# A two-block transformer in one kernel: attention's turns and scores inside units, memory units split ahead of a norm, a third query unit ahead of the keys' turn

## The chip, the cores and the metric

The kernel runs on one core of one Trainium2 chip. The metric is the device time in microseconds (us) of one execution, the median of several; three executions of the kernel before gave 1648.68, 1643.34 and 1647.32 us, median 1647.32 us.

## The reference, cut to what matters

The input is 256 tokens of width 1024, all float32. Two blocks follow each other.

- The first block has two layers (here L = 0 and 1). Each has a mixer with three branches on one input projection (a long convolution by spectra, differential attention with 4 heads, pooling), an output projection, a layer norm, a mixture of experts with a gated side path, and a second layer norm.
- The second block has two layers (here 2 and 3). Layer 2 mixes by a gated MLP with a spatial product. Layer 3 is a latent attention: projected and normed queries of 512, projected and normed keys and values of 256, 8 heads of 192 (128 plain and 64 rotated), causal. Both also attend to a memory of 256 rows, whose keys and values come from one product, `rms_norm(mem) @ w_mem_kv`, taken once. Both end in an RMS norm and a mixture of experts.

```
# differential attention, layers 0 and 1
probs = softmax(q1 k1) - lam * softmax(q2 k2);  heads = probs @ v
# memory, once
mem_kv = rms_norm(mem, g) @ w_mem_kv
# latent attention, layer 3
q = rms_norm(rms_norm(h @ w_q) @ w_q_up);  kv = rms_norm(h @ w_kv) @ w_kv_up
```

## The kernel before, in words

**Units.** All weights come as units of 1 MB (less in layer 3), 128 partitions by 2048. SyncE loads them in their order of use into a ring of 4 buffers (`RAW`); the load of a unit waits until VectorE has done with the unit four ahead of it. A float32 product is made of three fp32r products, so every unit is split: ScalarE copies it to a rounded high part (`w_hi`, L1423), VectorE subtracts that from the raw values to get the low part (`w_lo`, L1980), each in two halves (`split`). The parts have 3 buffers; ScalarE's `split` waits until TensorE has used the unit three before. TensorE takes a unit in `unit_by_token` (24 matmuls of 512 columns, L633 to L635) or `unit_by_channel` (48 matmuls of 256 columns, L679 to L681 and L633 to L635); it waits for the first half ahead of chunk 0 and for the second ahead of chunk 2. A callback `mid` runs in `unit_by_token` between chunks 1 and 2.

**Order.** Nothing plans at run time. Each engine's instruction list is written out by hand in one function for that engine, and it is worked off strictly in that order, with semaphores between the engines. On TensorE the 8 PSUM banks have owners: `claim(bank)` waits for the signal of whoever reads the bank last.

**Turns.** `turn` on TensorE transposes blocks into a bank (L650); ScalarE copies it out rounded (`t_hi`, L1429), VectorE subtracts for the low part (`t_lo`, L1992).

**Attention, layers 0 and 1.** Scores come in four rounds r = 0 to 3: `scores(r)` on TensorE (L948, banks 4 and 5 for even r, 6 and 7 for odd), `negmax(r)` on VectorE (L2471, L2474), `exponential(r)` on ScalarE (L1624), `weigh(r)` on VectorE (L2482 to L2488: the two softmaxes combined), `turn_probs(r)` on TensorE (L961), `probs_t(r)` on ScalarE (L1632: copies the transposed probabilities out). `scores(2)` needs the bank that `probs_t(0)` frees, `scores(3)` the one that `probs_t(1)` frees. TensorE's order before is: scores 0 and 1; the first unit of the third convolution strip; turn 0; scores 2; the second unit of that strip; turn 1; scores 3; a unit of the values strip; turn 2; the transposes of the convolution's input (L1066); the pooling products (L1075); the second unit of the values strip; turn 3. ScalarE's `conv_b` step (L1614) waits for the end of the second unit of the third convolution strip.

**Memory units, start of layer 2.** Four units carry `w_mem_kv`. TensorE works them as two strips (`strip((4, 5), ...)`, `strip((2, 3), ...)`, L1207 and L1208), then turns the normed activations (`turn(("n1", 2), ...)`, L1209) and starts layer 2's own units. Between the splits of these units VectorE makes layer 1's last norm (`shift_and_scale`, L2072, four instructions of 1024 columns), measures the result (L2045) and makes the RMS norm `n1` (`finish_rms`, L2063). It keeps the memory keys and values at L2677 and L2684, which wait for TensorE's second and fourth unit.

**Layer 3.** `unit_kv(0)` and `unit_kv(1)` make keys and values, `unit_q(0)` to `unit_q(3)` the queries, in 384 columns each, alternating between banks 0, 1 and 2, 3. ScalarE and VectorE work each in one `query_strip(i)`: copy the bank out, square it, sum the squares. TensorE's order before is: query unit 0, memory probabilities turn 0, query unit 1, turn 1, memory values 0, `k_nope` (the keys' turn, four groups in banks 5, 7, 5, 7), memory values 1, `k_rope`, query unit 2, the memory heads' turn, the first half of the queries' turn, query unit 3, scores. VectorE's `tables()` builds the rotation tables and also turns the 64 rotated key columns (L2816 to L2819), ahead of the copy of the memory queries (`z_m`, L2838).

Of the kernel before, what the change touches and what calls it, by code (L numbers as in the profile page):

```python
# [15 lines left out]
ALU = mybir.AluOpType  # L16
# [5 lines left out]
TB = T // P  # L22
# [114 lines left out]
def program(nc, A, seen):  # L137

    ctx = ExitStack()
    with ctx:  # L140
# [482 lines left out]
        def _(pe):  # L623
# [45 lines left out]
            def unit_by_channel(cells, pool_bank, first, last):  # L669

                pe.wait_ge(split_half[0], s.count(1))
                for c in range(4):
                    if c == 2:
                        pe.wait_ge(split_half[1], s.count(1))
# [256 lines left out]
            for L in range(DEPTH):  # L931
# [120 lines left out]
                turn_probs(0)  # L1052
                scores(2)
                unit_by_channel(cells_b, 3, False, True)
                owner[2], owner[3] = dve_ready.at(("conv_b", L)), evac_a.at(("pool", L))
                turn_probs(1)
                scores(3)
                claim(0, 1)
                unit_by_token((0, 1), lambda c: c, True, False)
# [245 lines left out]
            def unit_q(i):  # L1305
                banks = (2 * (i % 2), 2 * (i % 2) + 1)
                claim(*banks)
                unit_by_token(banks, lambda c: c, True, True, 384)
                owner[banks[0]], owner[banks[1]] = evac_a.at(("q_up", i)), evac_d.at(("q_up", i))
# [5 lines left out]
            mem_values(3, 0, ATC, 4)  # L1315
            turn("k_nope", lambda h: KV[:, :, 256 * h:256 * h + P], 8, [dve_ready.at("k")], low=False, banks=(5, 7))
            mem_values(3, 1, ATC, 6)
            turn("k_rope", KRP, 4, [], low=False, banks=(5, 7))
            unit_q(2)
# [92 lines left out]
        def _(act):  # L1412
# [184 lines left out]
            for L in range(DEPTH):  # L1597
# [71 lines left out]
                exponential(2)  # L1669
# [7 lines left out]
                split()  # L1677
                exponential(3)
# [81 lines left out]
            split()  # L1760
            root(("n1", 2), 2)
            split()
# [118 lines left out]
            split(4 * 384)  # L1881
            mem_probs_t(3, 0, ATC, (4, 5))

            def query_strip(i):
# [8 lines left out]
                act.nop().then_inc(*evac_a.tick(("q_up", i)))  # L1893
                act.wait_ge(*evac_d.at(("q_up", i)))
# [32 lines left out]
            query_strip(0)  # L1927
            mem_probs_t(3, 1, ATC, (6, 7))
            query_strip(1)
            turn("k_nope", 8, KTN, banks=(5, 7), scale=GNK[:, 2:3])  # L1930
            turn("k_rope", 4, KTR, banks=(5, 7))
            query_strip(2)
# [3 lines left out]
            query_strip(3)  # L1936
# [27 lines left out]
        def _(dve):  # L1964
# [424 lines left out]
            for L in range(DEPTH):  # L2389
# [142 lines left out]
                convolve("conv_a", range(4), lambda j: j // 2)  # L2532
                negmax(2)
                split()
# [135 lines left out]
            done("mem_root")  # L2670
            shift_and_scale(X, ("ln2", 1))
            done(("ln2", 1))
            measure(X)
            finish_rms(("n1", 2), None, GROW1, ("norm1", 2), split)
            split()
# [130 lines left out]
            def tables():  # L2806
# [6 lines left out]
                sync()  # L2813
                k1, k2 = ZB[:, :, 768:800], ZB[:, :, 800:832]
# [21 lines left out]
            done("tables")  # L2836
            used(first, 5)
            copy(ZB[:, 1, 832:1344], BK[1][:, :], "z_m")  # L2838
            turn("cq", 4, TH, TL, banks=(5, 6))
            split()  # L2840
# [14 lines left out]
            split(4 * 384)  # L2855
            mem_negmax(3, 0, (4, 5))
# [6 lines left out]
            variance("k")  # L2863
            split(4 * 384)
# [8 lines left out]

            def query_strip(i):

                used(first, 8 + i)
                b = 2 * (i % 2) + 1
                copy(QQ[:, 1, 384 * i:384 * i + 384], BK[b][:, 0:384], ("q_up", i))
                dve.wait_ge(*act_ready.at(("ssq", 4 + i)))
                go(dve.tensor_reduce(SQS[:, :].rearrange("p (b h) -> p b h", b=TB)[:, :, 2 * i:2 * i + 2],  # L2880
                                     SCR[:, :].rearrange("p (b n) -> p b n", b=TB)[:, :, 0:384]
                                     .rearrange("p b (h c) -> p b h c", c=192), X_AXIS, ALU.add))
                done(("ssq", i))
# [47 lines left out]
            query_strip(0)  # L2931
            split(4 * 384)
            mem_heads(3, 0, 4, CATM)
            query_strip(1)
            rotate(0)
            mem_heads(3, 1, 6, CATM)
            query_strip(2)
            turn(("heads_m", 3), 4, TH[:, 4:8, :], TL[:, 4:8, :], banks=(4, 6))
            split()
            query_strip(3)  # L2940
# [109 lines left out]
```

## Time and profile before

| | |
|---|---|
| median of three executions | 1647.32 us |
| the profiled execution | 1646.45 us |
| its span in the trace | 1644.4 us |
| TensorE busy | 1523.8 us (93%) |
| VectorE busy | 1316.9 us (80%) |
| ScalarE busy | 1029.5 us (63%) |
| mean granted TensorE clock | 0.973 of full |
| DMA, mean | 244 GB/s |

A row of the timeline gives the start, the duration, the engine, the line, the operation with its tiles and the number of instructions merged; in brackets stands how long the engine had been idle before it and what ended that. A busy matrix engine is not one at its peak, and the ends of its matmuls are modelled. The granted clock is 1.0 (2.4 GHz) or 0.5 (1.2 GHz); a mean between them says how much of a stretch was at either.

### The profile page before, as it was taken

The page shows a single profiled execution, that of the slowest core. Times are in us where ns is not written, and L with a number is a line of the kernel's source. Part 1 is how long each engine was busy: PE and PEld are TensorE (multiplying, and loading weights), DVE is VectorE, ACT ScalarE, POOL GpSimd, SP SyncE. Part 2 cuts the span into 40 slices and gives each one's busy share as a digit, 9 for nine tenths or more (in the row PEclk, how much of TensorE's full clock was granted, in tenths as well). Part 3 has the DMA queues.
Part 4 walks back from the last instruction along what each step waited for, and adds up shares of the span by engine and source line. Part 5 has one row for each costly group of instructions (what it writes and reads, how often), then busy time and mean ns, then how long its engine had stood idle before and what let it go on. Part 6 is the DMA issues. An engine that isn't in the chain of part 4 may idle for free.

```text
span 1644.4 us, 21331 instructions
## 1 busy us (share of the span) xinstructions
PE 1523.8 (93%) x7238; PEld 1245.9 (76%) x7238; DVE 1316.9 (80%) x1945; ACT 1029.5 (63%) x1499; POOL 94.3 (6%) x185
## 2 busy tenths in 40 slices
PE   7999999979899999989969999999789969999998
PEld 4777877858778778768858888887677758788886
DVE  5767899887678999866677999988875568899897
ACT  3544677745546777547436777776575437777775
POOL 4002000030022000000200000000000200000000
PEclk9999999989999999999979999999999979999999
DMA  8533599965437899745537999999441419999996
GB/s 280 163 109 121 183 336 348 332 213 192 138 105 225 296 340 332 263 156 166 169 104 241 360 360 360 362 321 353 153 146 60 132 52 306 350 361 359 361 333 232
DMA packets 307455, 401.79 MB, mean 244 GB/s; under 512 B 16028, under 2 KB 220540, under 8 KB 307092
## 3 DMA queue, kind: packets, MB, share of 16 engines
q1 hardware_dynamic: 298500, 382.00, 70.2%
q0 software_dynamic: 8848, 18.43, 3.9%
q8 instruction: 58, 0.95, 0.2%
q14 instruction: 49, 0.40, 0.1%
HBM read 399.33 MB, written 1.05 MB: 243 GB/s over the span
## 4 chain that ended last, share of the span: by engine, by line
PE 73%; DVE 16%; ACT 5%; DMA 4%; issue 2%; DVEq 0%; SPq 0%; ACTq 0%; POOLq 0%
PE bank L633 20%; PE bank L635 19%; PE bank L634 19%; DVE w_lo_at L1980 6%; DMA raw_at<-in_moe_w_up_dram 2%; PE bank L650 2%; ACT w_hi_at L1423 2%; PE bank L773 1%; PE bank L800 1%; PE bank L938 1%; DMA raw_at<-in_moe_w_dram 1%; DVE x_at L2355 1%; DVE t_lo_at L1992 1%; DVE x_at L2010 1%; DVE x_at L2016 1%
## 5 line engine op out<-in xcount | busy, mean ns | idle before, releaser
L1980 DVE TENSOR_TENSOR w_lo_at<-raw_at,w_hi_at 128x1024 fp32r<-128x1024 f32 (+1 forms) x730 | 853.8, 1212 | 102.5 <-ACT w_hi_at L1423 93.4
L1423 ACT ACTIVATE w_hi_at<-raw_at 128x1024 fp32r<-128x1024 f32 (+1 forms) x730 | 726.8, 1046 | 176.0 <-PE bank L635 79.2
L633 PE MATMUL bank<-w_hi_at,xs_hi_at 128*128 128x512 f32 x800 | 325.7, 407 | 15.3 <-DVE w_lo_at L1980 7.6
L635 PE MATMUL bank<-w_hi_at,xs_lo_at 128*128 128x512 f32 x800 | 316.4, 395 | 0.0
L634 PE MATMUL bank<-w_lo_at,xs_hi_at 128*128 128x512 f32 x800 | 314.1, 393 | 0.0
L633 PE MATMUL bank<-w_hi_at,t_hi_at 128*128 128x512 f32 (+3 forms) x528 | 208.2, 394 | 14.4 <-DVE t_lo_at L1992 8.5
L635 PE MATMUL bank<-w_hi_at,t_lo_at 128*128 128x512 f32 (+3 forms) x528 | 201.6, 382 | 0.0
L634 PE MATMUL bank<-w_lo_at,t_hi_at 128*128 128x512 f32 (+3 forms) x528 | 201.5, 382 | 0.0
L633 PEld LDWEIGHTS bank<-w_hi_at,xs_hi_at 128*128 128x128 f32 x800 | 151.6, 189 | 47.9 <-DVE w_lo_at L1980 9.5
L635 PEld LDWEIGHTS bank<-w_hi_at,xs_lo_at 128*128 128x128 f32 x800 | 151.5, 189 | 35.3
L634 PEld LDWEIGHTS bank<-w_lo_at,xs_hi_at 128*128 128x128 f32 x800 | 152.1, 190 | 30.7
L633 PE MATMUL bank<-w_hi_at,act_hi_at 128*128 128x512 f32 x384 | 154.2, 402 | 3.9 <-DVE act_lo_at L2244 3.9
L634 PE MATMUL bank<-w_lo_at,act_hi_at 128*128 128x512 f32 x384 | 151.6, 395 | 0.0
L635 PE MATMUL bank<-w_hi_at,act_lo_at 128*128 128x512 f32 x384 | 151.4, 394 | 0.0
L633 PEld LDWEIGHTS bank<-w_hi_at,t_hi_at 128*128 128x128 f32 x528 | 100.8, 191 | 39.3 <-issue 18.0
L635 PEld LDWEIGHTS bank<-w_hi_at,t_lo_at 128*128 128x128 f32 x528 | 100.8, 191 | 18.6
L634 PEld LDWEIGHTS bank<-w_lo_at,t_hi_at 128*128 128x128 f32 x528 | 101.0, 191 | 16.8 <-issue 0.5
L633 PEld LDWEIGHTS bank<-w_hi_at,act_hi_at 128*128 128x128 f32 x384 | 72.2, 188 | 24.6 <-issue 7.0
L635 PEld LDWEIGHTS bank<-w_hi_at,act_lo_at 128*128 128x128 f32 x384 | 72.4, 189 | 17.2
L634 PEld LDWEIGHTS bank<-w_lo_at,act_hi_at 128*128 128x128 f32 x384 | 72.5, 189 | 15.5
L1496 ACT ACTIVATE act_hi_at<-bank 128x256 fp32r<-128x256 f32 x96 | 36.6, 381 | 61.3 <-PE bank L800 60.9
L1429 ACT ACTIVATE t_hi_at<-bank 128x512 fp32r<-128x512 f32 x47 | 26.3, 596 | 61.7 <-PE bank L650 61.7
(505 smaller groups left out, 1734.7 us busy)
## 6 DMA issues: line engine op xcount, KB each, us to landing
raw_at<-in_moe_w_dram SPq DMA_DIRECT2D x192, 512.0 KB, 5.9
raw_at<-in_moe_w_gate_dram SPq DMA_DIRECT2D x128, 512.0 KB, 5.9
raw_at<-in_moe_w_up_dram SPq DMA_DIRECT2D x128, 512.0 KB, 7.6
raw_at<-in_moe_w_down_dram SPq DMA_DIRECT2D x128, 512.0 KB, 6.2
raw_at<-in_w_in_dram SPq DMA_DIRECT2D x40, 512.0 KB, 5.5
raw_at<-in_a_w_in_dram SPq DMA_DIRECT2D x20, 512.0 KB, 4.6
raw_at<-in_w_out_dram SPq DMA_DIRECT2D x16, 512.0 KB, 4.2
raw_at<-in_ple_wg_dram SPq DMA_DIRECT2D x16, 512.0 KB, 5.7
```

What stands on the lines that cost most here:

```text
L633: pe.matmul(out, ah, bh, start=start, stop=False, skip_group_check=loose)
L634: pe.matmul(out, ah, bl, start=False, stop=False, skip_group_check=loose)
L635: return pe.matmul(out, al, bh, start=False, stop=stop, skip_group_check=loose)
L650: ins = pe.transpose(BK[b][:, c * T + tb * P:c * T + tb * P + P], block_, IDENT)
L773: ins = pe.matmul(BK[2 * tb + half][:, :], ST[:, tb * P:(tb + 1) * P], y[:, half * 512:half * 512 + 512], start=first and y is YH, stop=False,
L800: ins = pe.transpose(BK[6 + e % 2][:, f * P:(f + 1) * P], GLU[:, f * P:(f + 1) * P], IDENT)
L938: ins = pe.matmul(out, mat[:, kb, cols], rhs(kb), start=kb == 0, stop=kb == 1)
L1423: act.activation(WH[:, s.part(), a], RAW[:, s.slot(), a], ACT.Copy).then_inc(hi_half[i], 1)
L1429: act.activation(dst[:, 2 * g:2 * g + 2, :], BK[banks[g % len(banks)]][:, :].rearrange("p (c t) -> p c t", c=2), ACT.Copy, scale=scale)\
L1496: act.activation(AH[e % 2][:, :, :], BK[6 + e % 2][:, 0:256].rearrange("p (c t) -> p c t", t=P), ACT.Copy).then_inc(*m.ah.tick())
L1980: dve.tensor_tensor(WL[:, s.part(), a], RAW[:, s.slot(), a], WH[:, s.part(), a].bitcast(F32), ALU.subtract).then_inc(split_half[i], 1)
L1992: dve.tensor_tensor(dl[:, 2 * g:2 * g + 2, :], BK[banks[g % len(banks)]][:, :].rearrange("p (c t) -> p c t", c=2), dh[:, 2 * g:2 * g + 2, ...
```

## The change

In the attention of layers 0 and 1, `turn_probs(0)` moves into the middle of the second convolution unit, `scores(2)` behind that unit, and `scores(3)` into the middle of the first values unit. ScalarE makes `exponential(2)` behind the next split instead of ahead of `conv_b`; VectorE makes its next split ahead of `negmax(2)`. At the start of layer 2, both split the third and the fourth memory unit earlier: VectorE one ahead of `shift_and_scale` and one ahead of `measure`, ScalarE both ahead of `root(("n1", 2), 2)`. In layer 3, `unit_q(2)` moves ahead of `k_nope`; `query_strip` is cut into `query_block` (copy out and first square) and `query_squares` (second square, sum); and the rotated keys move out of `tables()` to behind the turn of `cq`.

```diff
             def unit_by_channel(cells, pool_bank, first, last, mid=None):
...
                 for c in range(4):
+                    if c == 2 and mid is not None:
+                        mid()
...
# TensorE, layers 0 and 1
-                turn_probs(0)
+                unit_by_channel(cells_b, 3, False, True, mid=lambda: turn_probs(0))
+                owner[2], owner[3] = dve_ready.at(("conv_b", L)), evac_a.at(("pool", L))
                 scores(2)
-                unit_by_channel(cells_b, 3, False, True)
-                owner[2], owner[3] = dve_ready.at(("conv_b", L)), evac_a.at(("pool", L))
                 turn_probs(1)
-                scores(3)
                 claim(0, 1)
-                unit_by_token((0, 1), lambda c: c, True, False)
+                unit_by_token((0, 1), lambda c: c, True, False, mid=lambda: scores(3))
                 turn_probs(2)
# TensorE, layer 3
             mem_values(3, 0, ATC, 4)
+            unit_q(2)
             turn("k_nope", ...)
             mem_values(3, 1, ATC, 6)
             turn("k_rope", KRP, 4, [], low=False, banks=(5, 7))
-            unit_q(2)
# ScalarE, layers 0 and 1
                 probs_t(0)
-                exponential(2)
                 (conv_b, pool)
                 probs_t(1)
                 split()
+                exponential(2)
                 exponential(3)
# ScalarE, start of layer 2
             root(("ln2", 1), 4)
             split()
+            split()
             root(("n1", 2), 2)
-            split()
# ScalarE, layer 3
-            split(4 * 384)
-            mem_probs_t(3, 0, ATC, (4, 5))
...
+            query_block(0)
+            mem_probs_t(3, 0, ATC, (4, 5))
+            split(4 * 384)
+            query_squares(0)
             mem_probs_t(3, 1, ATC, (6, 7))
-            query_strip(1)
+            query_block(1)
+            query_squares(1)
+            query_block(2)
             turn("k_nope", 8, KTN, banks=(5, 7), scale=GNK[:, 2:3])
             turn("k_rope", 4, KTR, banks=(5, 7))
-            query_strip(2)
+            query_squares(2)
# VectorE, layers 0 and 1
+                split()
                 negmax(2)
-                split()
                 convolve("conv_b", (4, 5), lambda j: 2)
# VectorE, start of layer 2
             done("mem_root")
+            split()
             shift_and_scale(X, ("ln2", 1))
             done(("ln2", 1))
+            split()
             measure(X)
-            finish_rms(("n1", 2), None, GROW1, ("norm1", 2), split)
-            split()
+            finish_rms(("n1", 2), None, GROW1, ("norm1", 2))
# VectorE, layer 3
             tables()
-            done("tables")
             used(first, 5)
             copy(ZB[:, 1, 832:1344], BK[1][:, :], "z_m")
             turn("cq", 4, TH, TL, banks=(5, 6))
+            turned_keys()
+            done("tables")
...
             variance("k")
+            query_block(0)
             split(4 * 384)
             rooted("k", 16)
...
-            query_strip(0)
+            query_squares(0)
             split(4 * 384)
             mem_heads(3, 0, 4, CATM)
-            query_strip(1)
+            query_block(1)
+            query_squares(1)
             rotate(0)
+            query_block(2)
             mem_heads(3, 1, 6, CATM)
-            query_strip(2)
+            query_squares(2)
```

## Rows read from the trace of the kernel before

**Rows 1.** The page, the chain that ended last, by engine.
```profile
PE 73%; DVE 16%; ACT 5%; DMA 4%; issue 2%; DVEq 0%; SPq 0%; ACTq 0%; POOLq 0%
```

**Rows 2.** TensorE by stretch: length, busy (count), granted clock, DMA share, GB/s.
```profile
73.40:79.40 6.00, 6.00 (x50) 1.00 0.86 294
85.30:92.90 7.60, 7.60 (x50) 0.74 0.21 71
420.20:427.50 7.30, 7.30 (x50) 0.77 0.12 20
704.70:718.40 13.70, 13.70 (x48) 0.79 0.85 291
722.40:733.40 11.00, 10.97 (x48) 1.00 0.45 143
```

**Rows 3.** Timeline of TensorE, attention of layer 0.
```profile
80.35 0.66 PE L961 MATMUL bank<-consts_at,probs_a_at 128*128 128x128 f32 x4 [0.92 <-DVEq L2490]
83.33 2.08 PE L948 MATMUL bank<-qkt_at 64*128 64x256 f32 x8 [2.32 <-ACT at_a_at L1632]
95.17 1.13 PE L948 MATMUL bank<-qkt_at 64*128 64x256 f32 x8 [1.65 <-ACT at_a_at L1632]
96.24 0.50 PE L633 MATMUL bank<-w_hi_at,t_hi_at 128*128 128x512 f32 x1
101.82 0.60 PE L961 MATMUL bank<-consts_at,probs_a_at 128*128 128x128 f32 x4
```

**Rows 4.** Timeline of TensorE, attention of layer 1.
```profile
416.05 0.66 PE L961 MATMUL bank<-consts_at,probs_a_at 128*128 128x128 f32 x4 [0.78 <-DVEq L2490]
419.12 1.13 PE L948 MATMUL bank<-qkt_at 64*128 64x256 f32 x8 [2.41 <-ACT at_a_at L1632]
```

**Rows 5.** Timeline of ScalarE, attention of layer 0.
```profile
80.79 2.00 ACT L1423 ACTIVATE w_hi_at<-raw_at 128x1024 fp32r<-128x1024 f32 x2 [0.18 <-ACT probs_a_at L1624]
82.70 0.58 ACT L1632 ACTIVATE at_a_at<-bank 128x512 f32<-128x512 f32 x1
```

**Rows 6.** Timeline of VectorE, attention of layer 0.
```profile
82.44 3.35 DVE L2498 SCALAR_TENSOR_TENSOR uc_at<-bank,cols_at,uc_at 128x255 f32<-128x255 f32 x8
97.00 0.17 DVE L2482 RECIPROCAL r_at<-su_at 128x2 f32<-128x2 f32 x1 [0.17 <-DVE vvt_at L2536]
98.79 1.29 DVE L2471 TENSOR_REDUCE mx_at<-bank 128x2 f32<-128x512 f32 x2
```

**Rows 7.** The chain in order of time: one round of exponentials.
```profile
78.67 1.94 ACT probs_a_at L1624 x8
```

**Rows 8.** Timeline of TensorE, memory units and first unit of layer 2.
```profile
704.66 0.79 PE L633 MATMUL bank<-w_hi_at,xs_hi_at 128*128 128x512 f32 x1 [5.63 <-DVE w_lo_at L1980]
722.43 0.49 PE L633 MATMUL bank<-w_hi_at,t_hi_at 128*128 128x512 f32 x1 [2.11 <-DVE t_lo_at L1992]
```

**Rows 9.** Timeline of VectorE, start of layer 2.
```profile
694.81 2.48 DVE L2072 SCALAR_TENSOR_TENSOR x_at<-x_at,mv_at,row_at 128x1024 f32<-128x1024 f32 x2 [0.18 <-DVE rs_mem_at L2669]
703.38 2.36 DVE L1980 TENSOR_TENSOR w_lo_at<-raw_at,w_hi_at 128x1024 fp32r<-128x1024 f32 x2 [0.22 <-DVE rs_at L2039]
718.61 0.75 DVE L2684 TENSOR_SCALAR mem_v_at<-bank,rs_mem_at 128x512 f32<-128x512 f32 x1 [4.53 <-PE bank L635]
719.82 2.48 DVE L1992 TENSOR_TENSOR t_lo_at<-bank,t_hi_at 128x512 fp32r<-128x512 f32 x4 [0.46 <-ACT t_hi_at L1429]
```

**Rows 10.** Timeline of TensorE, layer 3.
```profile
1197.72 0.47 PE L633 MATMUL bank<-w_hi_at,t_hi_at 128*128 128x512 f32 x1 [1.17 <-DVE zb_at L2617]
1232.06 1.97 PE L650 MATMUL bank<-consts_at,kv_at 128*128 128x128 f32 x8 [3.82 <-ACT ktn_at L1429]
1245.47 0.63 PE L650 MATMUL bank<-consts_at,qrp_at 128*128 128x128 f32 x4 [1.78 <-DVE t_lo_at L1992]
```

**Rows 11.** Timeline of ScalarE, the keys' turn of layer 3.
```profile
1231.34 1.25 ACT L1429 ACTIVATE ktn_at<-bank,gnk_at 128x512 f32<-128x512 f32 x2
```

**Rows 12.** Who waited for whom: us in total, times, longest.
```profile
ACT w_hi_at L1423 <- DMA raw_at<-in_moe_w_up_dram: 38.2, 63, 2.3
```

More of the change, by code:

```diff
@@ L667, in unit_by_token, with unit_by_channel @@
                 s.unit += 1
-            def unit_by_channel(cells, pool_bank, first, last):
+            def unit_by_channel(cells, pool_bank, first, last, mid=None):
                 pe.wait_ge(split_half[0], s.count(1))
                 for c in range(4):
+                    if c == 2 and mid is not None:
+                        mid()
                     if c == 2:
@@ L1880, in _, with query_block @@
             root("k", 16)
-            split(4 * 384)
-            mem_probs_t(3, 0, ATC, (4, 5))
-            def query_strip(i):
+            def query_block(i):
                 used(first, 8 + i)
@@ L1893, in query_strip, with query_squares @@
                 act.nop().then_inc(*evac_a.tick(("q_up", i)))
+            def query_squares(i):
                 act.wait_ge(*evac_d.at(("q_up", i)))
@@ L1935, in _ @@
             turn_queries(0, (5, 7, 4))
-            query_strip(3)
+            query_block(3)
+            query_squares(3)
             root("q", 16)
@@ L2813, in tables, with turned_keys @@
                 sync()
+            def turned_keys():
                 k1, k2 = ZB[:, :, 768:800], ZB[:, :, 800:832]
@@ L2855, in _, with query_block, query_squares @@
             split(4 * 384)
+            def query_block(i):
+                used(first, 8 + i)
+                b = 2 * (i % 2) + 1
+                copy(QQ[:, 1, 384 * i:384 * i + 384], BK[b][:, 0:384], ("q_up", i))
+            def query_squares(i):
+                dve.wait_ge(*act_ready.at(("ssq", 4 + i)))
+                go(dve.tensor_reduce(SQS[:, :].rearrange("p (b h) -> p b h", b=TB)[:, :, 2 * i:2 * i + 2],
+                                     SCR[:, :].rearrange("p (b n) -> p b n", b=TB)[:, :, 0:384]
+                                     .rearrange("p b (h c) -> p b h c", c=192), X_AXIS, ALU.add))
+                done(("ssq", i))
             mem_negmax(3, 0, (4, 5))
@@ L2872, in _ @@
             done("k")
[L2874 to L2883, printed above, removed]
             def rotate(half):
@@ L2929, in heads @@
                 ins.then_inc(*heads_taken.tick((mla, r)))
-            query_strip(0)
+            query_squares(0)
             split(4 * 384)
             mem_heads(3, 0, 4, CATM)
-            query_strip(1)
+            query_block(1)
+            query_squares(1)
             rotate(0)
+            query_block(2)
             mem_heads(3, 1, 6, CATM)
-            query_strip(2)
+            query_squares(2)
             turn(("heads_m", 3), 4, TH[:, 4:8, :], TL[:, 4:8, :], banks=(4, 6))
             split()
-            query_strip(3)
+            query_block(3)
+            query_squares(3)
             plus_eps(RS[:, :], SQS[:, :], 192)
```

## The prediction

> **What bounds the kernel now.** I read the chain that ended last first: 73% of it is TensorE, 16% VectorE, 5% ScalarE and 4% transfers [rows 1]. So what counts is where TensorE stands still or runs at its lower clock, and who ends that. Then I went through TensorE's timeline at the three places that the change touches, looking at the brackets for idle time, and asked the view by stretches for the granted clock around them. The reader is to see two losses that come together. In attention TensorE idles 0.92, 2.32 and 1.65 us in layer 0 [rows 3] and 0.78 and 2.41 us in layer 1 [rows 4], where a third gap of the same 1.65 us follows. Right behind, the second convolution unit takes 7.6 us at a mean clock of 0.74 and 7.3 us at 0.77, while the same 50 rows took 6.0 us at 1.00 [rows 2]: part of it ran at 1.2 GHz instead of 2.4. The memory units show the same: 5.63 us idle [rows 8], then 48 matmuls in 13.7 us at 0.79, against 11.0 us at 1.00 for the same number later [rows 2]. A gap of 2.11 us ahead of that later stretch [rows 8] cost no clock.
>
> **Attention, layers 0 and 1.** Nothing is added or removed; the order changes. From the end of the first convolution unit (80.35 less 0.92, 79.43 us) to turn 2 (101.82 us) layer 0 takes 22.4 us [rows 3]. The work in it at full clock is one unit by channel 6.0 [rows 2], two turns of 0.6, two rounds of scores of 1.1 (1.13 where the clock was full), one unit by token 5.6 (96.24 to 101.82) [rows 3]: 15.0 us. The change takes out, in gaps and clock, 0.92 + 2.32 + 1.65 + (2.08 - 1.13) + (7.6 - 6.0) = 7.4 us, if nothing new is late. In layer 1: 0.78 + 2.41 + 1.65 + (7.3 - 6.0) = 6.1 us [rows 2, 4]. A matmul behind a change of kind takes 0.50 us instead of 0.39, so the two insertions cost some 0.1 us each; the transition existed before too, and I leave it out.
>
> What could be late next, in layer 0's times. Turn 0 comes 3 us into the second unit, at 82.4, and its weights are ready at 80.3, when TensorE took them before [rows 3]. Scores 2 wait for ScalarE's copy of turn 0: its split ends at 82.8, the copy takes 0.58 [rows 5], so 83.6 against the unit's end at 79.4 + 6.0 + 0.6 = 86.0. Scores 3 stand in the middle of the values unit, at some 90.5; ScalarE's conv_b and pool step (three copies of half a bank or a whole one, taken at the 0.58 of a whole one) and its copy of turn 1 end at about 88.5. The tight one is turn 2, which TensorE wants at 79.4 + 15.0 = 94.4. ScalarE: 88.3, split 2.0 [rows 5] to 90.3, the exponentials 1.94 [rows 7] to 92.3. VectorE: first convolution to 85.8 [rows 6], split 2.36 [rows 9] to 88.3, negmax 1.29 [rows 6] and its small step to 89.8, so it does not hold the exponentials. `weigh` takes from 97.00 to 98.79, 1.8 us with its waits [rows 6], so 94.1 plus handovers of 0.1: 94.2 to 94.5. I take 0.1 us of waiting a layer. Each further handover may add 0.1 to 0.2, so up to 1.5 us a layer. Round 3 has more room: between turn 2 and turn 3 lie a whole unit and the pooling products. Sum for attention: 7.4 + 6.1 - 0.2 = 13.3 us, bounds 10.5 and 13.5. VectorE's split stands ahead of negmax, so the loads behind it start earlier, not later; POOL's parameter loads hang on scores 3 and turn 3 and move along.
>
> **Memory units.** VectorE's list carries this place. Before, from 694.81 (shift_and_scale) to the end of the measured statistics (703.38 less 0.22, 703.16) is 8.35 us [rows 9]. Two splits now stand within it, 2.3 us each where they follow other work: statistics at 707.8. Root and reciprocal 0.5, `finish_rms` 2.48 as its shape in [rows 9]: the norm is done at 710.9 (before: 708.4). Behind it memory keys 0.75, one split 2.36, memory values 0.75 [rows 9] and small ones 0.3 bring 715.2, the four low parts 2.48: 717.7. TensorE's first own unit of layer 2 starts at 717.8 instead of 722.43 [rows 8], 4.6 us earlier. That the fourth memory unit ends much sooner (its split is there at 704.7, so it runs 704.8 to 710.5, not to 718.4) gives nothing of itself: TensorE turns `n1` by about 713 and then stands for some 4.5 us where it stood 2.11. What hides the two splits is TensorE's third unit, which is no longer late; what is late next is VectorE's row of keys, split, values, low parts.
>
> That gap is between the 2.11 us that cost no clock and the 5.63 us that did [rows 8], and nearer to the 3.2 us (0.92 and 2.32) of attention, that did too. So I expect the clock to fall: not at all is 0 us, a stretch like the one behind the 5.63 us lost 13.7 - 11.0 = 2.7 us [rows 2], with all of it behind the gap some 3.4. I take 2.4. The memory units then give 4.6 - 2.4 = 2.2 us, bounds 1.2 and 4.6.
>
> The Trainium skill speaks against this part. "TensorE: Matmul & The Clock Gate", section "What's actually happening", says that the lower rate is the default state and that activity lifts it, so a longer idle stretch is paid again in the matmuls behind it. By it alone the part is worth its lower bound, and without it the 4.6. The trace agrees in kind: 0.79 behind 5.63 us idle.
>
> **Layer 3.** The copy `z_m` no longer stands behind the six small operations on the keys; TensorE idled 1.17 us for it [rows 10] and now gets 1.05 of that. The six go behind the turn of `cq`, so the next split is 0.6 us later, hidden behind the 5.7 us of key unit 0 (0.6 us if that were gone). Query unit 2 fills the wait for the keys' turn. Before, the third group of keys waited 3.82 us for ScalarE's first copy [rows 10], made at 1231.34 [rows 11]. After, ScalarE has to do block 1, squares 1 and block 2 first (its engine is in order, and block 2 reuses the scratch that VectorE frees with the sum of round 1). I followed both engines through this and get the first copy of the keys at 1231.4 with the 1.05 us in it: no gain there, the third group starts at 1232.1 as before. The gain is behind it: query unit 2 is gone from there, 4.2 us (three quarters of a 5.6 us unit); eight transposes take 1.1 instead of 1.97 [rows 10], and the memory values behind them, in the same slow stretch, gain 1.0; the wait for the heads' low part shrinks from 1.78 [rows 10] to 1.0 as `query_squares(2)` is earlier; small waits give back 0.5. Sum 4.2 + 0.9 + 1.0 + 0.8 - 0.5 = 6.4, and query unit 3 and all behind it come that much earlier. Gaps of 2.2 and 1.0 us remain. The clock may fall for them (2.11 did not, 3.2 in two pieces did): 0 to 3.4 us, I take 0.7, as the row nearest to the larger gap had no fall. Layer 3: 5.7 us, bounds 2.9 and 6.4.
>
> **Sum.** 13.3 + 2.2 + 5.7 = 21.2 us. The profiled execution took 1646.45 us (span 1644.4), so 1625.2; its median is 0.9 above it, so 1626. Bounds of the parts: 10.5 + 1.2 + 2.9 = 14.6 and 13.5 + 4.6 + 6.4 = 24.5, that is 1633 and 1623; three executions before lay 5 us apart, so I widen to 1619 and 1634.
>
> **Rivals.**
> 1. The clock falls behind every remaining gap, at its dearest: memory units 1.2, layer 3 2.9, attention 13.3: 17.4 us, 1630. For it: every gap over 3 us here was followed by a fall. Against: the 2.11 us gap was not, and attention keeps no gap.
> 2. Layer 3's keys come later. ScalarE now waits for VectorE twice ahead of them; if each wait lasts 2 us more than I followed, the part gives 1 to 2 us: 17 us, 1630. Against: VectorE has idle time there.
> 3. Round 2 of attention is late. Its exponentials now stand behind a split and `conv_b`; at 2.5 us a layer the sum is 16.2, 1631. For: the margin is some 0.1 us.
> 4. The transfers eat it. If the expert stages are paced by transfers from a fixed start, the time stays at 1647. Against: a load waits for VectorE's split four units back, so the whole stream moves along, and the transfer share in the attention stretches is 0.21 and 0.12 [rows 2].
> 5. Slower. The order in which loads and splits interleave in the expert stages is set by how they are entered. ScalarE waits 38.2 us in 63 waits for the up weights alone [rows 12]; should these waits grow by more than 21 us (55%), the gain is eaten up, and at double the time is 1664. Against: entry is from a full ring in both kernels.
>
> **How the numbers follow.** Forecast 0.55 (its own range 1621 to 1630), rival 1 0.19, rival 2 0.10, rival 3 0.08, rival 4 0.04, rival 5 0.04. About 0.3% is what a measurement of this kernel can tell from no change, 5 us. Faster 0.92, within it 0.04, slower 0.04.
>
> **What would show it.** Attention: no bracket over 0.5 us on L961 and L948 between the convolution units and turn 2, the second unit in 6.0 us plus the turn, clock 1.00; turn 2 starts 15 us behind the first unit's end in both layers. Memory units: third and fourth back to back, then a gap of 4 to 5 us ahead of layer 2's first unit and a clock under 1 behind it. Layer 3: query unit 2 behind memory values 0, a gap of some 2 us ahead of the third keys' group, and query unit 3 some 6 us earlier against layer 3's start than before. The sum is wrong if the expert stages change length by more than 2 us each, or if turn 2 waits more than 1 us.

## The result, and the profile after

The changed kernel takes 1626.41 us (median of 4 executions, 1621.36 to 1627.03); the kernel before took 1645.33 beside it (median of 4). The ratio is 0.9877 [0.9857, 0.9897]: 1.2% faster. Forecast were 1626 us and a range of 1619 to 1634. The profiled execution took 1627.03 us, its span is 1624.9, its mean granted clock 0.972. A repeat (experiment 1) gave 1624.85.

That the time was met to 0.4 us is in part luck. The forecast took 21.2 us off a median of 1647.32; the measured gain is 18.9 us, off a median of 1645.33. Two differences of some 2 us cancel. The interval of the ratio stands for a gain of 17 to 23.5 us.

The page's chain that ended last, by engine, against [rows 1]:

```profile
PE 77%; DVE 16%; ACT 3%; issue 2%; DMA 1%; DVEq 0%; ACTq 0%; SPq 0%; POOLq 0%
```

TensorE's share of the chain grew from 73 to 77%: less of the end hangs on others.

**Attention.** TensorE's timeline of layer 0 from the second convolution unit on, against [rows 3] (start, duration, engine, line, operation, tiles, count; a bracket would be idle time ahead of it, and "..." marks rows left out):

```profile
82.43 0.60 PE L963 MATMUL bank<-consts_at,probs_a_at 128*128 128x128 f32 x4
...
85.83 1.13 PE L950 MATMUL bank<-qkt_at 64*128 64x256 f32 x8
86.89 0.66 PE L963 MATMUL bank<-consts_at,probs_a_at 128*128 128x128 f32 x4
...
90.22 1.14 PE L950 MATMUL bank<-qkt_at 64*128 64x256 f32 x8
94.43 0.66 PE L963 MATMUL bank<-consts_at,probs_a_at 128*128 128x128 f32 x4
```

No row has a bracket, and turn 2 starts at 94.43 instead of 101.82. Layer 1 has the same picture; its last turn against [rows 4]:

```profile
423.22 0.66 PE L963 MATMUL bank<-consts_at,probs_a_at 128*128 128x128 f32 x4
```

TensorE by stretch from the end of the first convolution unit to turn 2, layer 0 and layer 1, against [rows 2] (stretch, length, busy and count, granted clock, DMA share, GB/s):

```profile
79.60:94.40 14.80, 14.70 (x97) 1.00 0.31 100
408.50:423.20 14.70, 14.64 (x97) 1.00 0.30 94
```

Both run at 2.4 GHz throughout and stand still for 0.1 us in all. The second query and key unit ahead of attention starts 0.27 us later in layer 0 than before (60.68 against 60.41), so turn 2 is 7.66 us earlier against it; layer 1 gains 6.47 in the same way. Together 14.1 us.

Turn 2 has next to no margin. VectorE's last step of `weigh(2)` ends 0.11 us ahead of it, at 94.32, and in layer 1 at 423.11, again 0.11 ahead:

```profile
93.44 0.88 DVE L2494 SCALAR_TENSOR_TENSOR probs_a_at<-probs_a_at,rc_at 128x256 f32<-128x256 f32 x2
```

**Memory units.** TensorE at the start of layer 2, against [rows 8]:

```profile
698.85 0.66 PE L650 MATMUL bank<-consts_at,y_at 128*128 128x128 f32 x4 [1.13 <-DVEq L1978]
699.69 1.53 PE L650 MATMUL bank<-consts_at,y_at 128*128 128x128 f32 x12 [0.18 <-DVE mem_k_at L2684]
705.29 0.79 PE L633 MATMUL bank<-w_hi_at,t_hi_at 128*128 128x512 f32 x1 [4.07 <-DVE t_lo_at L1998]
```

VectorE in the same stretch, against [rows 9]: the norm's last step, memory keys, a split, memory values and the low parts, one behind the other.

```profile
696.23 2.48 DVE L2069 SCALAR_TENSOR_TENSOR y_at<-x_at,rs_at,gain_at 128x1024 f32<-128x1024 f32 x2
698.89 0.75 DVE L2684 TENSOR_SCALAR mem_k_at<-bank,rs_mem_at 128x512 f32<-128x512 f32 x1 [0.18 <-DVE y_at L2069]
699.55 2.35 DVE L1986 TENSOR_TENSOR w_lo_at<-raw_at,w_hi_at 128x1024 fp32r<-128x1024 f32 x2
...
702.03 0.74 DVE L2691 TENSOR_SCALAR mem_v_at<-bank,rs_mem_at 128x512 f32<-128x512 f32 x1
702.69 2.47 DVE L1998 TENSOR_TENSOR t_lo_at<-bank,t_hi_at 128x512 fp32r<-128x512 f32 x4
```

The first own unit of layer 2 is 17.14 us earlier than before, where layer 1's expert stage had ended 12.15 us earlier: 5.0 us from this part. Behind the gap:

```profile
705.30:719.00 13.70, 13.70 (x50) 0.80 0.57 191
```

The 48 matmuls of the first two units take 13.67 us to the end of the last one; counted in the same way they take 11.2 at the full clock (experiment 7). So some 2.5 us are given back.

**Layer 3.** TensorE at the keys' turn, against [rows 10]:

```profile
1217.98 1.24 PE L650 MATMUL bank<-consts_at,kv_at 128*128 128x128 f32 x8 [2.57 <-ACT ktn_at L1429]
1219.06 3.45 PE L1191 MATMUL bank<-mem_v_at,at_c_at 128*128 128x128 f32 x16
1222.30 1.22 PE L650 MATMUL bank<-consts_at,krp_at 128*128 128x128 f32 x8
...
1226.59 0.63 PE L650 MATMUL bank<-consts_at,qrp_at 128*128 128x128 f32 x4 [1.26 <-DVE t_lo_at L1998]
```

and ScalarE, which ends that gap, against [rows 11]:

```profile
1214.59 0.52 ACT L1895 ACTIVATE scr_at<-qq_at 128x384 f32<-128x384 f32 x1 [2.33 <-DVE qq_at L2623]
1216.25 0.49 ACT L1888 ACTIVATE qq_at<-bank 128x384 f32<-128x384 f32 x1 [1.14 <-DVEq L1978]
...
1217.24 1.27 ACT L1429 ACTIVATE ktn_at<-bank,gnk_at 128x512 f32<-128x512 f32 x2
```

ScalarE idles 2.33 us for VectorE's copy of block 1 and 1.14 for its sum, both ahead of the keys. The queries' turn (the last row of the TensorE fence) is 18.88 us earlier than before, layer 3's start 14.1: 4.8 us from this part.

**Where the 19.5 us of the span are.** Span of before less span of after is 1644.4 - 1624.9. Attention 14.1, memory units 5.0 less 2.5 of clock, layer 3 4.8; the expert stage of layer 1 is 1.0 us longer (537.27 to 682.13 before, 524.12 to 669.98 after); the rest (+0.6 behind layer 3, some -1.5 in small ones elsewhere) is within what executions of one kernel differ by.

### The profile page after: what moved, and what is told of

It is laid out like the page before. It is cut to its first block, busy times and chain, and to the rows that moved or that the text cites. A ratio compares the mean times of both kernels' runs of the same rounds, so it can differ in the third digit from the quotient of the medians.

```text
span 1624.9 us, 21333 instructions
## 1 busy us (share of the span) xinstructions
PE 1523.2 (94%) x7238; PEld 1246.8 (77%) x7238; DVE 1317.0 (81%) x1945; ACT 1030.2 (63%) x1499; POOL 94.5 (6%) x185
## 3 DMA queue, kind: packets, MB, share of 16 engines
HBM read 399.33 MB, written 1.05 MB: 246 GB/s over the span
## 4 chain that ended last, share of the span: by engine, by line
PE 77%; DVE 16%; ACT 3%; issue 2%; DMA 1%; DVEq 0%; ACTq 0%; SPq 0%; POOLq 0%
PE bank L633 21%; PE bank L635 21%; PE bank L634 21%; DVE w_lo_at L1986 5%; PE bank L650 2%; PE bank L775 1%; PE bank L802 1%; ACT w_hi_at L1423 1%; PE bank L940 1%; DVE uc_at L2504 1%; DVE y_at L2069 1%; DVE t_lo_at L1998 1%; DVE x_at L2361 1%; DMA raw_at<-in_moe_w_dram 1%; DVE x_at L2016 1%
```

## The experiments

The runs of the kernel before in the three groups of experiments had medians of 1645.94 (24 runs), 1646.18 (19) and 1646.21 (17).

**1. The change again.** No edit.

> The whole change once more, beside its parts on one chip. Theory (the three places add up and nothing is given back in the expert stages): 19 to 21 us under the kernel before. Rival (part of the gain is only another phase of the transfers or of the clock): another value than the first measurement's 18.9 us by more than 3 us.

Measured: 1624.85 us (5 runs), ratio 0.988 [0.9861, 0.99]. That is 19.7 us less by the ratio, as the theory had it. The memory gap is 4.08 us with a like fall of the clock behind it (0.79, against 0.80). The gap ahead of the third keys' group is 2.58 us, as in the first execution, but here nothing fell. TensorE by stretch, layer 3 and memory units:

```profile
1213.00:1225.50 12.50, 8.81 (x69) 1.00 0.25 85
703.00:716.50 13.50, 13.50 (x48) 0.79 0.54 180
```

So a gap of that length is followed by the lower clock in one execution and not in another. From the third keys' group to the queries' turn it takes 6.97 us here and 8.61 in the first execution.

**2. Attention alone.** The kernel before with the diff's edits of the attention on all three engines (TensorE's as in experiment 6), and nothing else.

```diff
 # ScalarE
-exponential(2)
 act.wait_ge(unit_used, s.count(-2))
...
 split()
+exponential(2)
 exponential(3)
 # VectorE
+split()
 negmax(2)
-split()
```

> Only the attention edits of layers 0 and 1. Theory: turn 2 starts 15 us behind the first convolution unit's end in both layers, and the time falls by the 7.4 and 6.1 us of gaps and lower clock that the trace of before showed, 12.5 to 14 us. Rival (the expert stages absorb it through their transfers): under 10 us, with the loss between turn 2 of one layer and the first norm of the next.

Measured: 1636.62 us (8 runs, 1631.58 to 1644.22), ratio 0.9939 [0.9918, 0.996], that is 6.6 to 13.5 us less. In place it does the whole of what it did in the changed kernel: 7.66 us in layer 0 and 6.47 in layer 1. The profiled execution took 1643.35 us, though, and lost elsewhere. TensorE behind layer 3's output turn, first this kernel:

```profile
1269.10 0.67 PE L1342 MATMUL bank<-ktn_at,qtn_at 128*128 128x256 f32 x2 [1.07 <-DVE t_lo_at L1992]
```

```profile
1269.00:1286.00 17.00, 16.90 (x43) 0.60 0.03 9
```

then the kernel before in the same place:

```profile
1277.90:1295.00 17.10, 17.02 (x76) 1.00 0.19 59
```

Behind 1.07 us of idle time TensorE ran most of 17 us at the lower clock and got through 43 instructions instead of 76. A mean clock of 0.60 over 17 us is 0.40 x 17 = 6.8 us lost; from this gap to the next wait of 1.65 us it takes 32.1 us, against 26.1 before. The same gap of 1.07 us stands here in all fourteen profiled executions of this document, and in the other thirteen the 17 us behind it ran at 1.00. So the gap alone does not bring the fall about, and what did is not known.

The expected 12.5 us or more is missed by the median. The rival had set under 10 us, as the median has it, with the loss between turn 2 of a layer and the next norm. The trace shows part of it there: up to layer 0's next norm turn (346.53) and to the end of layer 1's expert stage it takes 0.7 and 1.85 us more than before from turn 2 on, where the changed kernel takes 0.7 and 1.05 more. The larger losses stand in layers 2 and 3, which the edit does not touch: 6.1 us here, and 1.8 behind layer 2's first gap (last section).

**3. Memory units alone.** The kernel before with the diff's edits at the start of layer 2, of which VectorE's are

```diff
 # VectorE
+split()
 shift_and_scale(X, ("ln2", 1))
 done(("ln2", 1))
+split()
 measure(X)
-finish_rms(("n1", 2), None, GROW1, ("norm1", 2), split)
-split()
+finish_rms(("n1", 2), None, GROW1, ("norm1", 2))
```

> Only the memory units' splits. Theory: layer 2's first own unit starts 4.6 to 5 us earlier against the end of layer 1's experts, and about half of that is given back to the lower clock behind a gap of 4 us: 2.2 to 2.6 us in the end. Rival (the clock fall is the phase of one run): 4.5 to 5 us.

Measured: 1641.78 us (12 runs), 0.9979 [0.9965, 0.9993], that is 1.2 to 5.8 us less, median 4.2. Gap 4.08 us, the clock lower behind it. The interval holds both the expectation and its rival; the trace speaks for the expectation, since the clock fell (0.84 over the 11 us behind the gap).

**4. Layer 3 alone.** The kernel before with all edits of the diff in layer 3, of which TensorE's is

```diff
+unit_q(2)
 turn("k_nope", ...)
 mem_values(3, 1, ATC, 6)
 turn("k_rope", ...)
-unit_q(2)
```

> Only the edits of layer 3. Theory: 4.8 us, as query unit 3's start moved in the trace of the whole change against layer 3's start. Rival (it depends on the other parts through the clock's phase): between 3 and 6.5 us, with another granted clock behind the keys' gap.

Measured: 1640.44 us (11 runs), 0.9963 [0.9948, 0.9977], 3.8 to 8.6 us less, median 5.5. The gap is 2.55 us with the clock at 0.80 behind it, and from layer 3's first turn to the queries' turn it takes 79.7 us against 84.5 before: the expected 4.8. The whole change's other parts are not needed for it.

**5. Memory units and layer 3, without attention.** The edits of experiments 3 and 4 together.

> Memory and layer 3 edits together, attention as before. Theory (attention is worth 13 to 14 us in place, and attention alone came out at 9.3 us because its runs fell more often to the lower clock elsewhere): 7 to 9 us under the kernel before, so that the whole's 21 us leaves 12 to 14 us for attention. Rival (attention is really worth 9 us, the rest being lost in the expert stages): 11 to 12 us under the kernel before.

Measured: 1636.12 us (8 runs), 0.9946 [0.9927, 0.9964], 8.9 us less by its ratio. The whole change gives 19.7 by its ratio, so attention adds some 11 on top of the two, between its 14.1 in place and the 10.0 by ratio of experiment 2.

**6. The order on TensorE alone.** The edits of attention in TensorE's list; ScalarE and VectorE keep `exponential(2)` and `negmax(2)` where they were.

```diff
-turn_probs(0)
-scores(2)
-unit_by_channel(cells_b, 3, False, True)
+unit_by_channel(cells_b, 3, False, True, mid=lambda: turn_probs(0))
...
+scores(2)
 turn_probs(1)
-scores(3)
 claim(0, 1)
-unit_by_token((0, 1), lambda c: c, True, False)
+unit_by_token((0, 1), lambda c: c, True, False, mid=lambda: scores(3))
```

> The attention order of the whole change on TensorE alone; ScalarE makes the third round's exponentials ahead of conv_b and VectorE the split behind negmax(2), as before; memory units and layer 3 as before. Theory (moving the exponentials behind the split is needed): scores 3 in the middle of the values unit wait some 2 to 2.5 us for ScalarE's copy of turn 1, and turn 2 starts 17 to 18 us behind the first convolution unit's end instead of 15. Rival (TensorE's order alone does it): 15 us.

Measured: 1639.94 us (12 runs), 0.9969 [0.9951, 0.9987]. TensorE in this kernel:

```profile
91.30 1.13 PE L950 MATMUL bank<-qkt_at 64*128 64x256 f32 x8 [2.33 <-ACT at_a_at L1632]
95.22 0.60 PE L963 MATMUL bank<-consts_at,probs_a_at 128*128 128x128 f32 x4
...
421.74 2.08 PE L950 MATMUL bank<-qkt_at 64*128 64x256 f32 x8 [2.40 <-ACT at_a_at L1632]
```

ScalarE, which it waits for:

```profile
87.20 0.47 ACT L1624 ACTIVATE probs_a_at<-bank,nm_at 128x256 f32<-128x256 f32 x1 [4.87 <-DVE nm_at L2474]
...
89.25 1.02 ACT L1614 ACTIVATE uc_at<-bank,cols_at 128x256 f32<-128x256 f32 x2
...
90.64 0.60 ACT L1632 ACTIVATE at_a_at<-bank 128x512 f32<-128x512 f32 x1
```

`scores(3)` now waits 2.3 to 2.4 us in both layers for ScalarE's copy of turn 1 (90.64), which stands behind the exponentials of round 2, and these idle 4.87 us for the maxima of `scores(2)`. With ScalarE's and VectorE's edits this wait is gone (experiment 2). By the rows it is the exponentials ahead of `conv_b` that make it; a run with ScalarE's edit and without VectorE's was not made. Measured as above, from the second query and key unit to turn 2, TensorE's order alone gains 5.55 us in layer 0 and 1.20 in layer 1, where the clock fell too (the row at 421.74 has 2.08 us for scores that take 1.13): 6.8 of 14.1 us. By the ratios it is 5.1 us of experiment 2's 10.0. Turn 2 starts 17 us behind the first unit's end in layer 0, as expected, and 20 in layer 1, more than expected.

**7. The memory gap filled.** The changed kernel, and on TensorE, between the turn of `n1` and the wait for its low parts:

```diff
+claim(0, 1)
+for _ in range(30):
+    pe.transpose(BK[0][:, 0:P], IDENT, IDENT)
```

> The whole change, and TensorE makes 30 transposes of a constant into a free bank between the turn of the n1 activations and layer 2's first unit, where it otherwise stands for 4.07 us. They read and write nothing that is used. Theory (the lower clock behind the memory units follows from that gap): with some 3.7 us of work in the gap the stretch behind it runs at 1.00, its 48 matmuls take 11.0 us instead of 13.7, and the time falls by about 2.5 us against the whole change. Rival (the clock falls there for another reason, such as the work's kind): the 48 matmuls stay at 13.7 us and the time does not move.

and, a second time beside later kernels,

> The kernel with 30 transposes of the identity in the gap ahead of layer 2's first unit, once more, beside the two others. Theory (the 3 us gained there are given back in layer 2's expert stage by waits for transfers): 48 matmuls in 11.2 us at clock 1.00, norm 2 turned 3 us earlier, transfer waits in that stage over 30 us against 5, stage 3 us longer, time within 1 us of the changed kernel's. Rival (the first run's extra waits were a chance of that execution): transfer waits 5 to 15 us, stage 325 us, time 2.5 to 3 us under the changed kernel's.

Measured: 1626.1 us (6 runs), 0.9883 [0.9862, 0.9904], and 1626.2 (5 runs), 0.9863 [0.9841, 0.9885]. TensorE in the first of them:

```profile
698.26 3.44 PE L1212 MATMUL bank<-consts_at 128*128 128x128 f32 x30
702.50 0.49 PE L633 MATMUL bank<-w_hi_at,t_hi_at 128*128 128x512 f32 x1 [0.80 <-DVE t_lo_at L2001]
```

```profile
705.00:717.00 12.00, 12.00 (x59) 1.00 0.53 176
```

48 matmuls take 11.2 us instead of 13.7, so the 2.5 us are the clock's, and the idle time brought them about. From the turn of the memory rows to norm 2's turn it takes 153.7 us in both executions, against 156.2 and 156.6 in the changed kernel's two: 2.5 to 2.9 us gained. In the medians nothing of it is seen: the two are those of the changed kernel within 1.4 us. But each ratio is known to some 3.5 us only, and the second lies 2.3 to 2.8 us under the changed kernel's two, so a gain of 2.5 us is not refuted either. In the first execution layer 2's expert stage (from norm 2's turn to norm 3's) was 328.2 us long instead of 324.9, with these waits for weights in it:

```profile
ACT w_hi_at L1426 <- DMA raw_at<-in_moe_w_up_dram: 21.0, 32, 2.3
ACT w_hi_at L1426 <- DMA raw_at<-in_moe_w_down_dram: 15.6, 19, 2.0
```

In the second it was 325.7 with 15.3 us of such waits. The changed kernel had 30.8 us of them in one execution and 5.0 in the other at the same 324.9. So these waits don't measure what the stage loses, and "given back in the expert stage" held once and not twice. The profiled executions also differ ahead of the filling, where it can't act: from turn 2 of layer 0 to layer 1's second query and key unit, and from turn 2 of layer 1 to the turn of the memory rows, the second took 5.2 us more than the changed kernel's first execution, and the first 2.6 us less. That filling takes the fall away is shown; whether the 2.5 us arrive in the time of the whole kernel stays open.

**8. Both remaining gaps closed.** The changed kernel. Start of layer 2: `n1` is turned over four banks on all three engines, and VectorE takes its low parts ahead of the memory keys and values. Layer 3: ScalarE copies the keys ahead of query block 2, VectorE makes block 1 ahead of its split.

```diff
 # VectorE, layer 2
+split_part(0)
+turn(("n1", 2), DC, TH, TL, banks=(6, 7, 4, 0))
+split_part(1)
+s.unit += 1
 used(first, 1)
...
-split()
...
-turn(("n1", 2), DC, TH, TL)
 # ScalarE, layer 3
-query_block(2)
 turn("k_nope", 8, KTN, banks=(5, 7), scale=GNK[:, 2:3])
 turn("k_rope", 4, KTR, banks=(5, 7))
-query_squares(2)
 turn(("heads_m", 3), 4, TH[:, 4:8, :], banks=(4, 6))
+query_block(2)
+query_squares(2)
 # VectorE, layer 3
 query_squares(0)
-split(4 * 384)
-mem_heads(3, 0, 4, CATM)
 query_block(1)
+mem_heads(3, 0, 4, CATM)
 query_squares(1)
+split(4 * 384)
...
 mem_heads(3, 1, 6, CATM)
+turn(("heads_m", 3), 4, TH[:, 4:8, :], TL[:, 4:8, :], banks=(4, 6))
 query_squares(2)
-turn(("heads_m", 3), 4, TH[:, 4:8, :], TL[:, 4:8, :], banks=(4, 6))
```

> The whole change, and: VectorE makes the low parts of the n1 turn right behind the norm and half a split, with its memory keys and values behind them (the turn uses banks 6, 7, 4, 0); in layer 3 ScalarE copies the keys' turn and the memory heads' turn ahead of query_block(2), and VectorE makes query_block(1) and mem_heads ahead of the split. Theory: layer 2's first unit starts 2.5 to 3 us earlier and its gap shrinks to 2 us with no fall of the clock (2.5 us), the keys' third group waits under 0.6 us instead of 2.57 (2 us and up to 1.2 of clock): 6 to 8 us under the whole change. Rival (each gap comes back at the next wait): under 3 us.

Measured: 1618.08 us (5 runs, 1615.27 to 1621.26), 0.9828 [0.9806, 0.985]: faster than both kernels, 7 to 8 us under the changed one's two medians and clear of its interval. In the trace the memory gap is 2.04 us with 1.00 behind it, the third keys' group waits 0.34 us, and from layer 3's first turn to the queries' turn it takes 74.9 us. Of what these places gained the profiled execution had less at the end, since layer 3's expert stage took 324.8 us against 321.9 in the changed kernel; why is not known.

**9 and 10. Each of the two alone.** The layer 2 edit:

> The changed kernel with one edit at the start of layer 2: the turn of n1 uses four banks (6, 7, 4, 0) and VectorE takes it ahead of its keeping of the memory keys and values. Both theories: the gap ahead of layer 2's first unit is 2.0 us instead of 4.1, its 48 matmuls take 11.0 us at clock 1.00 instead of 13.7, the first unit starts 3 to 4 us earlier, and norm 2 is turned 5 to 7 us earlier. Theory (a transfer-bound expert stage gives back only what exceeds its slack): 3 to 4 us under the changed kernel, 1621. Rival (layer 2's expert stage is paced by its transfers from a fixed start, as the filled gap suggested): the waits on up and down transfers in that stage rise from 5 to over 35 us, the stage is 3 us longer or more, and the time stays within 1.5 us of the changed kernel's 1625.

Measured: 1622.66 us (5 runs), 0.9854 [0.9831, 0.9876].

```profile
699.76 1.97 PE L650 MATMUL bank<-consts_at,y_at 128*128 128x128 f32 x16 [1.09 <-DVEq L1978]
703.76 0.49 PE L633 MATMUL bank<-w_hi_at,t_hi_at 128*128 128x512 f32 x1 [2.04 <-DVE t_lo_at L1998]
```

```profile
703.70:715.00 11.30, 11.24 (x51) 1.00 0.71 231
```

The gap is 2.04 us, the clock stays, and from the turn of the memory rows to norm 2's turn it takes 151.3 us, 4.9 us less than in the changed kernel. The expert stage behind is 324.9 us long, with 18.1 us of waits on up and down weights: what this edit gained was not taken back there. The median is 2 to 4 us under the changed kernel's two. The trace speaks for the theory and against the rival's longer stage; the intervals of the ratios overlap, so the time alone does not decide between 3 to 4 us and "within 1.5". The layer 3 edit:

> The changed kernel with one edit in layer 3: the keys' turn is copied out ahead of query block 2, and VectorE makes query block 1 and the memory heads ahead of its split. Theory (the 2.6 us gap ahead of the third keys' group and the 2.3 us that ScalarE waited for block 1 are what was left, and layer 3 has no transfer that it outruns): gap 0.3 us, no fall of the clock, queries' products 6 to 9 us earlier against layer 3's start than in the changed kernel's own profiled run with its fall, time 3.5 to 5 us under it, 1620.5. Rival (block 2 is late instead and query unit 3 waits for the banks): 0 to 1.5 us under it.

Measured: 1622.8 us (6 runs), 0.9858 [0.9835, 0.988].

```profile
1212.51 1.24 PE L650 MATMUL bank<-consts_at,kv_at 128*128 128x128 f32 x8 [0.34 <-ACT ktn_at L1429]
1213.59 1.95 PE L1191 MATMUL bank<-mem_v_at,at_c_at 128*128 128x128 f32 x16
...
1218.56 0.63 PE L650 MATMUL bank<-consts_at,qrp_at 128*128 128x128 f32 x4 [0.19 <-DVE t_lo_at L1998]
```

Gap 0.34 us, and from layer 3's first turn to the queries' turn 74.9 us, against 79.7 and 80.8 in the changed kernel's two executions: 4.8 to 5.9 us, under the 6 to 9 expected in place, and 2 to 4 in the median, with intervals that overlap here too. The two edits together (4 to 8 us) agree with what experiment 8 measured.

**11. The rotated keys alone.** The kernel before with the six operations on the rotated keys behind the turn of `cq`.

```diff
 tables()
-done("tables")
 used(first, 5)
 copy(ZB[:, 1, 832:1344], BK[1][:, :], "z_m")
 turn("cq", 4, TH, TL, banks=(5, 6))
+turned_keys()
+done("tables")
```

> The kernel before with one edit: the six small operations on the rotated keys stand behind the turn of cq instead of ahead of the copy of the memory queries. Theory: TensorE's 1.17 us wait ahead of key unit 0 shrinks to 0.1, all behind comes 1.05 us earlier, time 1.0 us less (ratio 0.9994). Rival (the next split is now 0.6 us later and TensorE waits for it): 0.5 us less or nothing.

Measured: 1644.01 us (12 runs), 0.999 [0.9976, 1.0003]; the interval holds both 1 us and nothing. In the trace TensorE's wait of 1.17 us is gone, and the third keys' group starts 1.09 us sooner behind layer 3's first turn (70.03 us against 71.12). The queries' turn has only 0.27 us of that left (84.26 against 84.53). TensorE between the two, first this kernel and then the kernel before:

```profile
1231.00:1245.20 14.20, 12.44 (x72) 0.80 0.15 58
```

```profile
1232.00:1245.40 13.40, 11.62 (x72) 0.84 0.17 64
```

The same 72 instructions took 0.8 us more, at the lower clock for longer behind the same gap of 3.82 us. The theory holds as far as the third keys' group; what follows is the clock's, not the rival's later split.

## Why the prediction was right

**Attention, forecast 13.3, measured 14.1.** The order of the chain held: TensorE's own work fills the path but for `weigh(2)`, which the prediction had named as the tight one (94.2 to 94.5 forecast, 94.32 measured). The second unit had the clock at 1.00, and turn 2 started 14.8 us behind the first unit where 15.0 had been summed; TensorE stood still for 0.1 us in all, as forecast. The measured gain is 0.8 above the forecast and 0.6 above its upper bound, because the way from the first unit's end to turn 2 took 14.8 and 14.7 us where 15.1 had been set: the rows' durations, which had been added up, overlap by 0.1 to 0.2 us where one kind follows another. Experiment 6 confirms the step on which the margin rested: with `exponential(2)` left ahead, a wait is there. Over the whole kernel attention's share was smaller, about 11 by experiments 1 and 5. Experiment 2's execution shows one such loss, to the clock in a later stage; that this is where the rest went in the others is not shown.

**Memory units, forecast 4.6 - 2.4, measured 5.0 - 2.5.** The row that is late next was VectorE's keys, split, values, low parts: the gap of 4.07 us ends with the last low part, and the fall came. It came in all five executions with this gap (4.07 to 4.08 us; the 11 us behind it ran at 0.72 to 0.85), and with the gap filled in experiment 7 it did not. (The working has 717.7 for the end of the low parts; the terms that it lists make 717.5, and the measured one, shifted by the 12.15 us, is 717.3. The forecast does not hang on it.) The Trainium skill, "TensorE: Matmul & The Clock Gate", section "What's actually happening", says that the lower rate is the default and that activity lifts it; this trace agrees, with 0.80 behind 4.07 us.

**Layer 3, forecast 6.4 - 0.7, measured 4.8.** The keys' first copy came when it was said to, with no gain: the third group started 71.12 us behind layer 3's first turn both before (1232.06 less 1160.94) and after (1217.98 less 1146.86). The term for the clock was mis-sized: behind the gap of 2.57 us the memory values took 3.45 us, 1.5 more than the 1.95 where the clock was full (experiments 1 and 10), where 0.7 had been set. The prediction had counted them as 1.0 faster than the 3.07 before. The wait for the heads' low part was 1.26, not 1.0. Where the clock held, in experiment 1, the stretch from the third group to the queries' turn is 6.4 us shorter than before (6.97 against 13.41), just the forecast's sum without its clock term. The 0.7 rested on one gap of 2.11 us that cost nothing, and that was luck of one execution (last section). The part's lower bound of 2.9 should read 3.0 (6.4 less 3.4).

**The sum.** Forecast 21.2 us. The parts as measured make 14.1 + 2.5 + 4.8 = 21.4, and the profiled executions differ by 1646.45 - 1627.03 = 19.4: some 2 us were lost in stages that the change doesn't touch, of which 1.0 is layer 1's expert stage.

**The rivals.** Rival 1 had half of its case: the clock fell behind both remaining gaps, but at its dearest in neither; its 17.4 us lie under the measured 18.9 to 19.7, though still in the interval. That was the first execution; in the second the clock held behind the keys' gap and fell for longer at layer 3's start. Rival 2 (keys later) and rival 3 (round 2 late) are refuted by the rows above. Rival 4 and 5: layer 0's and layer 2's expert stages kept their length within 0.6 us and layer 1's grew by 1.0, so neither a fixed pace nor longer waits took the gain. Over all fourteen profiled executions layer 2's expert stage was 324.2 to 328.2 us long and layer 3's 320.8 to 324.8, so a few us can be lost there in a single one.

## What to carry to other kernels

When one engine is the bound and others hand it small pieces, put each small piece in the middle of a long one, and move on the other engines what stands ahead of its copy: the order on the bound engine alone gave about half here (6.8 of 14.1 us in place, 5.1 of 10.0 by the ratios). A gap that such a reordering leaves or moves is worth closing by order, because the clock can fall behind it: two further edits of the lists bought another 7 us, while filling the gap with idle products kept the clock but showed no gain in the medians. Compare stages by their own start and end in the trace, and sum them; the total alone can't tell 2 us here.

## What the runs showed of the hardware that was not expected

The spread between executions goes with the clock. Over the 60 runs of the kernel before the span and the mean granted clock correlate at -0.92, and the span grows by 1.17 us for each 0.001 less of clock, between 0.975 and 0.966. No edit is behind it, since it is one kernel, and from the fastest span to the slowest it is 12 us, more than the memory units' and layer 3's parts together. Whether the clock makes the whole of it is not shown.

The length of a slow stretch is not given by the gap ahead of it. Ahead of layer 3's first turn TensorE idles 7.8 us in every kernel here. The 16.1 us from that turn on, first in the changed kernel, then in its repeat:

```profile
1146.80:1162.90 16.10, 14.55 (x81) 0.87 0.74 225
```

```profile
1144.50:1160.60 16.10, 14.51 (x69) 0.65 0.75 225
```

The same gap cost 0.13 of 16.1 us in one and 0.35 in the other: 2.1 and 5.6 us. The gap of 2.55 to 2.58 us ahead of the third keys' group was followed by the lower clock in six executions of seven: in the changed kernel and in experiments 4, 5, 7 (both) and 9 (0.80 over the 8.6 us behind it), and not in experiment 1. Nor is the gap of 2.11 us ahead of layer 2's first unit free, as the prediction had taken it from one row. Five kernels have it, with the same order of work around it. The 11 us behind it ran at 1.00 in [rows 2] and at 0.84 in the other four, those of experiments 2, 4, 6 and 11; here 2 and 4:

```profile
710.50:721.50 11.00, 10.99 (x41) 0.84 0.45 148
```

```profile
721.10:732.10 11.00, 10.96 (x41) 0.84 0.44 144
```

which is 1.8 us lost in each. So part of what the layer 2 edit gave in the single executions of experiments 8 and 9, at 1.00 behind 2.04 us, may not come in every execution. One and the same gap came out 1.8, 3.5 and, in experiment 2, over 6 us apart from one execution to another: a single trace does not price an idle gap better than that.
